# First loads split by use, and the joints between dense stages reworked, in a two-layer decoder step on one core

## What is computed

```python
for i in range(DEPTH):                                   # DEPTH = 2
    if i % 2 == 0:
        mix = delta_mixer(x, ...)                        # x @ w_in, conv, chunked delta rule, @ w_out
    else:
        mix = shortconv_mixer(x, ...)                    # x @ w_in, conv, @ w_out
    x = layer_norm(ALPHA * x + mix, ln_mix_g[i], ln_mix_b[i])
    f = conv_ffn(x, ...)                                 # x @ w_up, width-3 conv, silu gate, @ w_down
    x = layer_norm(ALPHA * x + f, ln_ffn_g[i], ln_ffn_b[i])
    x = x + (p[i] @ ple_w_proj[i]) * sigmoid(x @ ple_w_gate[i])
```

## Time and profile before

| what | value |
|---|---|
| median of three runs | 1806.93 us |
| the profiled execution: its time, and its span | 1807.6 us, 1805.8 us |
| PE busy | 1745.5 us (97%) |
| DVE busy | 1131.7 us (63%) |
| ACT busy | 457.5 us (25%) |
| POOL busy | 286.0 us (16%) |
| moved by DMA | 139.36 MB, 77 GB/s on average |

### The profile page before, as it was taken

One profiled execution on the slowest core, in us unless ns is written; L12 is line 12 of the kernel. 1 busy time (PEld: TensorE's weight loads), 2 busy tenths in 40 slices (PEclk: granted clock), 3 DMA queues, 4 the chain that ended last, 5 costly groups with the idle time before them and its releaser, 6 DMA issues. The chain is left out here.

```text
span 1805.8 us, 21924 instructions
## 1 busy us (share of the span) xinstructions
PE 1745.5 (97%) x7699; PEld 1358.2 (75%) x7699; DVE 1131.7 (63%) x2177; ACT 457.5 (25%) x1092; POOL 286.0 (16%) x582
## 2 busy tenths in 40 slices
PE   8999999998899999999999999989899999999999
PEld 5677789985667777777776777766677777777767
DVE  4756787859776766773337655557776676643365
ACT  2433406633232222220004101112322222200041
POOL 0111106545320000000112000003200000001120
PEclk9999999999999999999999999999999999999999
DMA  4232210024112222242130222211122222331211
GB/s 148 71 110 83 78 59 13 1 106 152 47 48 82 82 71 82 82 141 84 65 106 24 94 70 81 84 57 47 47 71 83 82 71 82 124 106 71 94 37 53
DMA packets 45340, 139.36 MB, mean 77 GB/s; under 512 B 4896, under 2 KB 12192, under 8 KB 45232
## 3 DMA queue, kind: packets, MB, share of 16 engines
q1 hardware_dynamic: 41504, 132.90, 22.4%
q10 hardware_dynamic: 3728, 5.07, 0.9%
HBM read 129.63 MB, written 8.31 MB: 76 GB/s over the span
## 5 line engine op out<-in xcount | busy, mean ns | idle before, releaser
L269 PE MATMUL bank<-z,ring 128*128 128x288 f32 x1952 | 509.8, 408 | 8.4 <-DVE z L367 3.4
L269 PEld LDWEIGHTS bank<-z,ring 128*128 128x128 f32 x1952 | 372.0, 191 | 115.6 <-issue 3.5
L269 PE MATMUL bank<-x,ring 128*128 128x288 f32 x1632 | 431.0, 412 | 10.1 <-DMA x<-in_x 6.2
L269 PEld LDWEIGHTS bank<-x,ring 128*128 128x128 f32 x1632 | 313.3, 193 | 102.8 <-issue 13.6
L1994 DVE SCALAR_TENSOR_TENSOR scratch<-scratch 128x592 f32<-128x592 f32 x176 | 146.3, 832 | 25.5 <-ACT scratch L1938 23.9
L269 PE MATMUL bank<-y,ring 128*128 128x288 f32 x616 | 156.8, 406 | 3.0 <-DVE x L1776 2.0
L269 PEld LDWEIGHTS bank<-y,ring 128*128 128x128 f32 x616 | 116.8, 190 | 36.3 <-issue 2.4
L269 PE MATMUL bank<-big,ring 128*128 128x288 f32 x536 | 136.6, 410 | 6.8 <-issue 5.3
L269 PEld LDWEIGHTS bank<-big,ring 128*128 128x128 f32 x536 | 102.5, 192 | 36.8 <-issue 8.6
L2028 POOL COPY scratch<-scratch 128x2 f32<-128x2 f32 x88 | 26.0, 295 | 462.5 <-ACT scratch L1924 462.5
L1938 ACT ACTIVATE scratch<-scratch 128x592 f32<-128x592 f32 x88 | 69.4, 789 | 91.0 <-DVE scratch L1968 89.6
...
## 6 DMA issues: line engine op xcount, KB each, us to landing
...
```

The lines of the kernel that those rows point to most:

```text
L269: last = pe.matmul(bank[:, 0:HALF], w[:, k * P:(k + 1) * P], rhs(k), start=start and k == 0, stop=k == self.depth - 1, skip_group_check=no ...
```

## The change

In the front, x is alone on ACT's queue, in five loads: the first two tiles of its first quarter, the other two, then the other quarters. SP's queue begins with the first half of row 0 of both pairs (all that p1 needs), their second halves, the two other rows, and then WBA, KEEP, CV, IDENT and the states; the four masks follow behind the third pair's rows. p1(0) waits by parts, and the gate logits no longer wait for the constants.

At the joints:

- `inverse` of half 0 goes from DVE to ACT: Ln and then Exp with scale -0.5 take the place of Sqrt and reciprocal. `root_table` brings the Sqrt table back with a dummy activation. Half 1 keeps Sqrt and reciprocal.
- The last of the 16 result tiles is no longer added by POOL and DVE; PE takes it in with one more matmul for each of the two sums of half 1.
- In half 1 POOL subtracts the mean from all eight tiles, DVE from none.
- DVE's order around both halves is another, and weight sums of the next stage move in front of the norm of half 1 or into its gaps. ACT runs `deviation` ahead of the second `copy_s1`.
- In the up projection `p6_both` runs p6(0) and p6(1) together, step by step as `token2` is made.
- In the input gate the first four projections use banks 0, 1, 2 and 4. They wait no longer for the last read of bank 5. ACT copies the first two between the affines of half 0, the others between and behind those of half 1; p6(0) waits for 14 copies instead of 16.

Left out of the diff are the new semaphores and their waits for the first loads, the renumbered counts (15 sums and 13 squares for each norm in place of 16 and 14), and POOL's lists.

```diff
@@ -313,6 +318,20 @@
+    def p6_both(self, pe):
+        for i in range(2):
+            pe.wait_ge(sum2_made, self.base + i + 1)
+            if self.base + i >= 2:
+                pe.wait_ge(c21_read, self.base + i - 1)
+        for k in range(self.depth):
+            pe.wait_ge(token2_made, self.token_base + k + 1)
+            for i in range(2):
+                last = self.run(pe, BANK[2 + (self.base + i) % 2], i, "s2", self.t(2), True, None, (k,))
+                if k == self.depth - 1:
+                    last.then_inc(product6, 1)
@@ -1132,7 +1151,7 @@
-    return lambda pe, k: pe.wait_ge(x_in[2 * group + half], 16)
+    return lambda pe, k: pe.wait_ge(x_first if 2 * group + half == 0 and k < 2 else x_in[2 * group + half], 16)
@@ -1145,6 +1164,7 @@
+    pe.wait_ge(const_in, const_n[0])
@@ -1205,7 +1225,6 @@
-    pe.wait_ge(const_in, const_n[0])
@@ -1410,6 +1429,7 @@
+    dve.wait_ge(x_first, 16)
@@ -1535,15 +1555,25 @@
-    for row_n in range(2):
-        for pair in range(2):
-            load_ring(sync, pair, row_n, w[2 * pair + row_n])
+    for pair in range(2):
+        at = 3 * pair * ROW
+        sync.dma_start(RING[:, at:at + ROW // 2], w[2 * pair][:, 0:ROW // 2]).then_inc(first_in[pair], 16)
+    for pair in range(2):
+        at = 3 * pair * ROW
+        sync.dma_start(RING[:, at + ROW // 2:at + ROW], w[2 * pair][:, ROW // 2:]).then_inc(w_loaded[2 * pair], 16)
+    for pair in range(2):
+        load_ring(sync, pair, 1, w[2 * pair + 1])
+    sync.dma_start(WBA, I["w_ba"]).then_inc(g_in, 16)
+    sync.dma_start(KEEP[gate_rows], I["keep"]).then_inc(g_in, 16)
+    for dst, name in ((CV, "columns"), (IDENT, "identity")):
+        sync.dma_start(dst[:], I[name]).then_inc(const_in, 16)
...
-    for dst, name in ((MASKT, "mask_decay"), (MASKS, "mask_sample"), (MASKL, "mask_levels"), (ONES, "ones")):
-        sync.dma_start(dst[:], I[name]).then_inc(late_in, 16)
...
+        if i == 2:
+            for dst, name in ((MASKT, "mask_decay"), (MASKS, "mask_sample"), (MASKL, "mask_levels"), (ONES, "ones")):
+                sync.dma_start(dst[:], I[name]).then_inc(late_in, 16)
@@ -1561,13 +1591,11 @@
-    for half in range(2):
-        for group in range(2):
-            load_x(act, group, half)
-    act.dma_start(WBA, I["w_ba"]).then_inc(g_in, 16)
-    act.dma_start(KEEP[gate_rows], I["keep"]).then_inc(g_in, 16)
-    for dst, name in ((IDENT, "identity"), (CV, "columns")):
-        act.dma_start(dst[:], I[name]).then_inc(const_in, 16)
+    act.dma_start(X[:, 0:2, 0:HALF], I["x"][:, 0:2, 0:HALF]).then_inc(x_first, 16)
+    act.dma_start(X[:, 2:KH, 0:HALF], I["x"][:, 2:KH, 0:HALF]).then_inc(x_in[0], 16)
+    load_x(act, 1, 0)
+    load_x(act, 0, 1)
+    load_x(act, 1, 1)
@@ -1807,7 +1838,7 @@
-    DVE_PIECES = 2
+    DVE_PIECES = (2, 0)
@@ -1822,14 +1853,22 @@
-        last = max(n for n in range(2 * DT) if self.residual.place[n][0] == half)
-        pe.wait_ge(y_added, 16 * L + last + 1)
+        r, end = self.residual, 2 * DT - 1
+        last = max(n for n in range(end) if r.place[n][0] == half)
+        pe.wait_ge(y_added, 15 * L + last + 1)
...
-        pe.matmul(BANK[6][:, 0:HALF], ONES[:], sum_y[:, cols], start=True, stop=True)
-        pe.wait_ge(sq_added, 14 * L + self.residual.adds.index(last) + 1)
-        pe.matmul(BANK[7][:, 0:HALF], ONES[:], sum_sq[:, cols], start=True, stop=True).then_inc(ln_sums, 1)
+        pe.matmul(BANK[6][:, 0:HALF], ONES[:], sum_y[:, cols], start=True, stop=not half)
+        if half:
+            r.made(pe, end)
+            pe.matmul(BANK[6][:, 0:HALF], ONES[:], r.piece(r.place[end][1], half), start=False, stop=True)
+        pe.wait_ge(sq_added, 13 * L + r.adds.index(last) + 1)
+        last = pe.matmul(BANK[7][:, 0:HALF], ONES[:], sum_sq[:, cols], start=True, stop=not half)
+        if half:
+            pe.wait_ge(squared, 16 * (L + 1))
+            last = pe.matmul(BANK[7][:, 0:HALF], ONES[:], SQ[r.nth_square(end) % 2], start=False, stop=True)
+        last.then_inc(ln_sums, 1)
@@ -1840,7 +1879,17 @@
-        act.activation(rs[:, cols], rs[:, cols], ACT.Sqrt, bias=eps_ln).then_inc(ln_std, 1)
+        if half:
+            act.activation(rs[:, cols], rs[:, cols], ACT.Sqrt, bias=eps_ln).then_inc(ln_std, 1)
+        else:
+            act.activation(rs[:, cols], rs[:, cols], ACT.Ln, bias=eps_ln).then_inc(ln_std, 1)
+            act.wait_ge(ln_std, at + 1)
+            act.activation(rs[:, cols], rs[:, cols], ACT.Exp, scale=-0.5).then_inc(ln_inverse, 1)
+    def root_table(self, act):
+        act.activation(CV[:, 154:155], eps_ln, ACT.Sqrt)
@@ -2037,17 +2088,24 @@
+    def bank(self, n):
+        return (0, 1, 2, 4)[n] if n < 4 else 2 + n % 4
...
-            pe.wait_ge(c21_read, self.dense.base)
-            pe.wait_ge(c12_read, self.dense.base - (1 if n % 4 < 3 else 0))
-            if n >= 4 or L:
-                pe.wait_ge(projected_out, 2 * DT * L + n - 3)
+            if n < 4:
+                pe.wait_ge(c11_read, self.dense.base)
+                pe.wait_ge(c12_read, self.dense.base - 1)
+            elif n in (5, 7):
+                pe.wait_ge(c21_read, self.dense.base)
+                pe.wait_ge(c12_read, self.dense.base)
+            if n >= 4:
+                pe.wait_ge(projected_out, 2 * DT * L + max(4, n - 3))
...
-                last = pe.matmul(BANK[2 + n % 4][:, 0:HALF], W_PROJ[:, m, k * P:(k + 1) * P],
+                last = pe.matmul(BANK[self.bank(n)][:, 0:HALF], W_PROJ[:, m, k * P:(k + 1) * P],
@@ -2346,8 +2404,11 @@
-    d.p6(pe, 0)
-    d.p6(pe, 1)
+    if sums:
+        d.p6_both(pe)
+    else:
+        d.p6(pe, 0)
+        d.p6(pe, 1)
@@ -2416,10 +2477,11 @@
+    pe.wait_ge(projected_out, 2 * DT * layer + 2)
...
-        pe.wait_ge(projected_out, 2 * DT * (layer + 1))
+        pe.wait_ge(projected_out, 2 * DT * (layer + 1) - 2)
@@ -2467,6 +2529,7 @@
+    n.root_table(act)
@@ -2474,8 +2537,8 @@
+    n.deviation(act, 1)
...
-    n.deviation(act, 1)
@@ -2512,18 +2575,23 @@
-    r.square(act, 15)
+        if m == 3:
+            gate[layer].projection(act, slice(0, 2))
+            r.square(act, 15)
+    n.root_table(act)
...
-    g.projection(act, slice(0, 4))
+    g.projection(act, slice(2, 4))
...
+    n.deviation(act, 1)
...
-    n.deviation(act, 1)
-    for m in n.ORDER[1]:
+    for j, m in enumerate(n.ORDER[1]):
...
-    g.projection(act, slice(4, None))
+        if j >= 4:
+            g.projection(act, slice(j, j + 1))
+    g.projection(act, slice(8, None))
@@ -2558,7 +2626,12 @@
-    second_half_dve(dve, norm[2 * layer], d)
+    def second_sums(step):
+        if step == 0:
+            d.sum2(dve, 1)
+        else:
+            d.sum3(dve, 1)
+    second_half_dve(dve, norm[2 * layer], d, second_sums)
@@ -2676,12 +2749,11 @@
+    n.centre_dve(dve, 0)
+    n.scale(dve, 0, slice(0, 4))
+    r.c12(dve, 3)
...
-    n.centre_dve(dve, 0)
-    n.inverse(dve, 0)
-    n.scale(dve, 0, slice(0, None))
-    r.c12(dve, 3)
-    r.add_square(dve, 15)
+    n.scale(dve, 0, slice(4, None))
@@ -2734,29 +2805,29 @@
-    next_dense.sums123(dve, 0)
...
+    next_dense.sum1(dve, 0)
...
+    r.c12(dve, 3)
...
+    next_dense.sum2(dve, 0)
+    next_dense.sum3(dve, 0)
...
-    r.c12(dve, 3)
-    r.add_square(dve, 15)
-    next_dense.sum2(dve, 1)
-    next_dense.sum3(dve, 1)
-def second_half_dve(dve, n, d):
+def second_half_dve(dve, n, d, between=lambda step: None):
...
-    n.centre_dve(dve, 1)
+    between(0)
...
-        if k < 2:
-            n.scale(dve, 1, slice(4 + 2 * k, 6 + 2 * k))
...
+        if k < 2:
+            n.scale(dve, 1, slice(4 + 2 * k, 6 + 2 * k))
+    between(1)
@@ -2772,8 +2843,8 @@
+    d.sums123(dve, 1)
...
-    d.sums123(dve, 1)
@@ -2898,12 +2969,12 @@
-    for x in range(12, 16):
+    for x in range(12, 15):
...
-    norm[2 * layer].centre_pool(pool, 1, slice(2, 8))
+    norm[2 * layer].centre_pool(pool, 1, slice(0, 8))
@@ -3090,12 +3160,12 @@
-        norm[1].centre_pool(pool, 1, slice(2, 8))
+        norm[1].centre_pool(pool, 1, slice(0, 8))
...
-        norm[3].centre_pool(pool, 1, slice(2, 8))
+        norm[3].centre_pool(pool, 1, slice(0, 8))
```

29 lines of the change are left out of this document (18 added, 11 removed).

## The result

The changed kernel takes 1789.84 us (median of four runs, 1788.98 to 1790.70) against 1807.58 for the kernel before, run beside it: ratio 0.9902, 95% interval 0.9885 to 0.9919. The profiled execution's span fell from 1805.8 to 1787.2, 18.6 us. The forecast was 1785, a gain of 22.

What follows compares the result with a forecast made beforehand. PE was busy 1745.5 of 1805.8 us, leaving about 60 us of idle to win. Terms 1.7 + 5.2 + 4.7 + 5.35 + 5.3 = 22.2 us off 1807.6 gave 1785.4, stated as 1785; range 1776 to 1792.

Steps and rivals of the forecast that it cites:

- The start: At the kernel's first loads: x lands sooner and the gate logits follow x, not the constants; 1.7 us, low end 0.4.
- Rival E: At the first loads: x ends as late as before, only the constants' wait goes, at most 0.4 us; 1786 us, chance 0.05.
- Half 0: In the two up joints, to p1(0): DVE loses the 1.94 us reciprocal and its later work comes sooner; 2.1 us each.
- The sums: Sums of half 1, up joints: four matmuls follow p1(0) without a wait, 3.9 us in place of 6.5; 2.6 each.
- Sums to token2: Up joints, from the sums of half 1 to the first token2: nothing won, 9.4 us against 9.25 before.
- p6 together: Up joints, p6(0) to p3(0): two matmuls for each token2, 12.2 us against 12.8; 0.6 us each.
- The gate joints: Down projection to gate, both layers: first projection to p6(0) 25.6 us against 30.95 and 30.9; 5.3 us each.
- B: Up joints win only 3 us: tokens come later, PE stands 2 us longer at each p6; 1789 to 1792, chance 0.15.
- C: ACT in half 0: each table switch costs its 1.28 us twice, 8.4 us back; 1793 us, chance 0.03.
- D: Half 1, exclusive port: POOL's subtractions and DVE's operations take turns, 1.24 us a pair; 1787 us, chance 0.03.
- A: Faster: slowed operations and low clock don't return, both up joints win near 8.5 us; 1777 to 1779, chance 0.12.
- F: Slower: p6_both leaves PE part idle, the clock stays at 1.2 GHz in the up joints; 1814 us, chance 0.03.

Runs made afterwards that it cites:

- old_loads: The changed kernel with the start's loads and waits of before (x in four DMAs on ACT's queue, whole rows and masks on SP's): 1790.11 us.
- recip0: The changed kernel with Sqrt on ACT and the reciprocal on DVE in half 0 again: 1792.02 us.
- copies_early: The changed kernel with ACT's copies of projections 4 to 8 one affine earlier in the gate joints: 1787.16 us.
- exp1: The changed kernel with Ln and Exp in half 1 as well, no reciprocal at all: 1788.56 us.

## Why the prediction was right, and where it was not

The measured time lies in the range, faster as forecast; 3.5 us of the 22.2 are missing. Three terms of the sum were sized too large, by 3.7 us together; the misses of the others nearly cancel.

**The start (1.7, got 0.71).** The failed step is "x lands behind 5.12 MB, 0.4 us sooner". The steps beside it held: SP was through first (POOL had the conv weights, the last of its first loads, at 16.27), and WBA was there, since the logits waited for x last. But I took the same rate from the start, and the new loads moved 0.24 MB less in the first 7 us (old_loads), so x came 0.26 us later in this trace, and in none of the ten kernels sooner than the 16.90 of before. The gain was the difference between the old wait for constants and x itself, 17.96 to 17.28. Rival E had this way right and the size, 0.4 at most, too low.

**Half 0 (2.1, got 1.4).** The failed step is "Then I walk on with the durations: three scales of 0.40". The row was of scales with POOL idle. I had not asked what ran beside the reciprocal that I took out; recip0 shows it: 1.4 in place of 1.94. The rest of the 2.1 is a wrong comparison. The walk's waits, 0.4, 1.0 and 0.75 us, were set against "some 4.3 of such waits before", but 4.3 is all that p5(2) to p1(0) took beyond four products of 1.94. The waits themselves were 1.65, 1.24 and 0.69, and the other 0.8 (a product behind a wait takes 2.18) is still there. Like against like the walk gives 1.4. Its waits agree with the trace (0.26, 1.25 and 0.68), the first of them partly by luck: p5(3) starts 2.44 us behind p5(2), and with the three scales 0.58 shorter PE would not have waited at all.

**The sums (2.6, got 2.59 and 1.76).** The first number is right: four matmuls behind p1(0) without a wait, 3.9 us. In the second joint the full 2.6 stood in the sum, though before it took 5.68 us there and not 6.5: the sums with ones, at the low clock in the first joint (494.79 to 496.87), took 1.07 us in the second. The 0.5 taken off that joint covers part of it. And the reason was only half the reason: of the two edits DVE's order did most.

**Sums to token2 (-0.1, got -0.3).** 9.4 forecast, 9.54 and 9.55 measured, with the terms right one by one. What I missed is that "nothing" was a loss given away: with DVE's two subtractions kept it takes 8.83.

**p6 together (0.6, got 0.65 and 1.45).** Right in the first joint, low in the second. The stretch spreads by 1.5 us with the clock (last section), so the agreement in the first shows little.

**The gate joints (5.3, got 4.7).** The failed step is "the ninth waits about 0.35 for ACT": it waits 0.74, as ACT's affines follow DVE's slowed scales, 0.97 us apart, and the copy stood behind one more of them. The wait costs 0.23 us beyond its own length, as a product behind a wait does in half 0, and that was not counted either: copies_early puts the joint at 25.26, 0.97 less, where the work alone had been counted as 25.2.

**The rivals.** B named the measured time but not the way: PE stands 3.56 us ahead of p6, no longer than forecast, and the up joints gave 4.3 each and not 3. C fell: two table loads in a row cost 1.28 each, and in exp1 another on the path costs 1.28 too. By the rule that the prediction quoted from the Trainium skill (ScalarE: Activation LUTs, What ACT_TABLE_LOAD costs) a drain stands beside each; the rows show none. D, the exclusive port, would have had POOL pay as much as DVE. POOL's subtraction takes 0.90 us against 0.84 while a scale takes 0.97 against 0.40, and a pair in turns would take 1.24. So the rule of the Trainium skill (SBUF — State Buffer, Who interferes with whom) fits in that the two meet, but not in that one shuts the other out. A and F didn't happen.
